# A decoder-layer kernel on one core: the first four adaLN weight chunks multiplied on TensorE in four column strips, and the weight stream started without a hold

## The reference

```
c_act = silu(c)                                   # c: (1, 1024)
mod   = c_act @ ada_w + ada_b                     # ada_w: 1024 x 6144
sh1, sc1, gt1, sh2, sc2, gt2 = split(mod, 6)      # 1024 each
h     = rmsnorm(x, norm_mix_g) * (1 + sc1) + sh1  # the modulated x
proj  = h @ w_in                                  # pool, q, k, v, z, rates and gates
...                                               # causal pooling and gated delta rule, residual
h     = rmsnorm(x, norm_ffn_g) * (1 + sc2) + sh2
x     = x + gt2 * moe(h)                          # top 4 of 32 experts, clamped SwiGLU
out   = rmsnorm(x, final_norm_g)
```

## Time and profile before

| what | value |
|---|---|
| median of three runs | 1480.12 us |
| profiled execution, its own time | 1478.27 us |
| its span, first to last instruction | 1476.7 us |
| TensorE busy, mean granted clock | 1327.4 us (90%), 0.971 |
| VectorE busy | 425.7 us (29%) |
| ScalarE busy | 175.0 us (12%) |
| moved by DMA | 484.38 MB, mean 328 GB/s |

### The profile page before, as it was taken

One profiled execution on the slowest core, in us unless ns is written; L12 is line 12 of the kernel. 1 busy time (PEld: TensorE's weight loads), 2 busy tenths in 40 slices (PEclk: granted clock), 3 DMA queues, 4 the chain that ended last, 5 costly groups with the idle time before them and its releaser, 6 DMA issues.

```text
span 1476.7 us, 17501 instructions
## 1 busy us (share of the span) xinstructions
PE 1327.4 (90%) x6612; PEld 673.9 (46%) x6612; DVE 425.7 (29%) x1020; ACT 175.0 (12%) x355; POOL 73.6 (5%) x67
## 2 busy tenths in 40 slices
PE   2799998989988899999899989998999899989996
PEld 1688866878876433333233323332333233323332
DVE  5588525363222421211121112111211121112112
ACT  1000111121201210110011001100110011001102
POOL 1010003333100000000000000000000000000000
PEclk8799989999999899999999999999999999999999
DMA  9968541010434199999999999999999999999994
GB/s 319 382 235 311 193 175 57 1 57 2 148 147 158 78 427 425 425 428 428 425 425 430 427 424 426 428 427 424 426 429 427 423 426 429 426 425 425 430 427 200
DMA packets 69510, 484.38 MB, mean 328 GB/s; under 512 B 4061, under 2 KB 4250, under 8 KB 35562
## 3 DMA queue, kind: packets, MB, share of 16 engines
q1 hardware_dynamic: 68448, 481.47, 79.3%
q0 software_dynamic: 560, 1.40, 0.4%
q10 hardware_dynamic: 474, 1.11, 0.2%
HBM read 482.92 MB, written 1.05 MB: 328 GB/s over the span
## 4 chain that ended last, share of the span: by engine, by line
DMA 50%; PE 43%; DVE 5%; ACT 1%; issue 1%; ACTq 0%; SPq 0%; DVEq 0%
DMA ring<-in_exp_w_dram 49%; PE bank L679 18%; PE bank L1041 12%; PE bank L1067 2%; PE bank L884 2%; PE bank L881 1%; PE bank L874 1%; DVE region_z L1181 1%; PE bank L1012 1%; PE bank L797 1%; PE bank L1079 1%; PE bank L701 1%; DMA work<-in_gdn_norm_g_dram 1%; DMA ring<-in_ada_w_dram 1%; PE bank L778 0%
## 5 line engine op out<-in xcount | busy, mean ns | idle before, releaser
L1041 PE MATMUL bank<-ring,work 128*64 128x512 f32 x2112 | 474.9, 598 | 63.7 <-DMA ring<-in_exp_w_dram 63.7
L1041 PEld LDWEIGHTS bank<-ring,work 128*64 128x64 f32 x2112 | 143.8, 137 | 391.1 <-issue 261.9
L1067 PE MATMUL bank<-ring,work 128*64 128x512 f32 x1056 | 233.9, 595 | 0.0
L679 PE MATMUL bank<-region_h,ring 128*128 128x256 f32 x832 | 187.4, 387 | 5.8 <-DVE region_h L1198 4.2
L679 PEld LDWEIGHTS bank<-region_h,ring 128*128 128x128 f32 x832 | 160.0, 194 | 29.4 <-DVE region_h L1198 4.3
L1067 PEld LDWEIGHTS bank<-ring,work 128*64 128x64 f32 x1056 | 72.9, 137 | 137.4 <-issue 137.4
L1510 DVE TENSOR_SCALAR work<-bank 128x256 f32<-128x256 f32 x66 | 27.6, 419 | 365.4 <-PE bank L1041 365.4
L638 ACT ACTIVATE work<-work 128x256 f32<-128x256 f32 x66 | 27.5, 416 | 782.6 <-DVE work L1510 782.6
L1537 DVE TENSOR_TENSOR work<-bank,work 128x512 f32<-128x512 f32 x33 | 22.8, 691 | 315.7 <-PE bank L1067 315.7
L1012 PE MATMUL bank<-qkv,work 128*64 128x512 f32 x272 | 65.7, 605 | 2.1 <-ACT qkv L614 2.1
L1079 PE MATMUL bank<-work 64*128 64x512 f32 x264 | 65.6, 615 | 0.8 <-DVE work L1537 0.8
(11 more groups left out here) (268 smaller groups left out, 958.1 us busy)
## 6 DMA issues: line engine op xcount, KB each, us to landing
ring<-in_exp_w_dram SPq DMA_DIRECT2D x198, 2048.0 KB, 24.0
ring<-in_w_in_dram SPq DMA_DIRECT2D x13, 2048.0 KB, 11.9
ring<-in_ada_w_dram SPq DMA_DIRECT2D x12, 2048.0 KB, 12.7
ring<-in_w_gdn_out_dram SPq DMA_DIRECT2D x2, 2048.0 KB, 7.8
ring<-in_w_out_dram SPq DMA_DIRECT2D x2, 2048.0 KB, 7.9
ring<-in_w_pool_out_dram SPq DMA_DIRECT2D x1, 2048.0 KB, 9.2
consts<-in_const_dram SPq DMA_DIRECT2D x1, 1153.0 KB, 6.4
region_x<-in_x_dram SPq DMA_DIRECT2D x2, 512.0 KB, 11.0
```

Source lines behind the costliest of these rows:

```text
L679: mm = nc.tensor.matmul(out_ap, w(k) if w else w_slot(n, j, k), rhs[:, k, :], start=(k == 0), stop=(k == kc - 1))
L1041: mm = nc.tensor.matmul(bank[b][h * SLOTS:(h + 1) * SLOTS, :], xT[:, c % 4, c // 4, :], slot_as(q, 2)[:, i, lo:lo + 512], start=False, sto ...
L1067: mm = nc.tensor.matmul(bank[2][o * SLOTS:(o + 1) * SLOTS, :], actT[:, b, c, h, :], slot_as(4 + b, 2)[:, h, lo:lo + 512], start=(b + h + c ...
```

## The change

- The wait of SyncE for the small rows is gone. `c` has a semaphore of its own (`c_in`), `ada_b` is issued by ScalarE, only the identity and the ones (128 KB) are loaded ahead of `x`, and the rest of the constants (2050 columns) follows the sixth chunk, under `tables_in`.
- The four `ada` chunks are cut otherwise: chunk q holds rows 256q to 256q+255 of the first 2048 columns, in pieces of 8 KB.
- `ada_rows` multiplies each on TensorE: the stationary operand is a column of `c_act` repeated 32 times, the moving one 512 weight columns, and the four groups of 512 columns go to the four 32-column strips of the array, all into bank 5. VectorE's sums over these chunks are gone; ScalarE copies bank 5 to `ada_row` (in unused columns of `qkv`), and four matmuls with four columns of the identity turn it into the 16 columns of `mod`.
- `c` is transposed by itself, the transposes of `x` go to banks 1, 2, 3 and 7, and the small rows are turned between the third and the fourth chunk.
- `vec_hT` is raised after each of the eight feature tiles, and the first eight matmuls of the first projection wait for one tile each.

The diff, cut to its core:

```diff
@@ sync @@
-            sp.dma_start(rows[ROW_C:ROW_C + 8, :], c.rearrange("b (r n) -> (b r) n", n=P)).then_inc(rows_in, 16)
-            sp.dma_start(rows[ROW_ADA_B:ROW_ADA_B + 48, :],
-                         ada_b.rearrange("l (r n) -> (l r) n", n=P)).then_inc(rows_in, 16)
-            sp.dma_start(consts[:, :], const).then_inc(const_in, 16)
+            sp.dma_start(rows[ROW_C:ROW_C + 8, :], c.rearrange("b (r n) -> (b r) n", n=P)).then_inc(c_in, 16)
+            sp.dma_start(consts[:, 0:2 * P], const[:, 0:2 * P]).then_inc(const_in, 16)
             for t in range(T):
                 sp.dma_start(xt[:, t, :], x[0, t * P:(t + 1) * P, :]).then_inc(x_in, 16)
-            sp.wait_ge(rows_in, 16 * 10)
...
+                if n == RING - 1:
+                    sp.dma_start(consts[:, 2 * P:CONST_W], const[:, 2 * P:CONST_W]).then_inc(tables_in, 16)
@@ chunks @@
-        chunks = [("ada", cut(ada_w, CW * i)) for i in range(4)]
+        chunks = [("ada", ada_w[0, 2 * P * q:2 * P * (q + 1), 0:2 * D].rearrange("(c p) n -> p c n", p=P))
+                  for q in range(4)]
@@ scalar @@
-            act.wait_ge(vec_cols, 1)
-            nc.scalar.activation(c_act[:, :], cols[:, ROW_C:ROW_C + 8], ACT.Silu).then_inc(act_c, 1)
+            act.wait_ge(pe_c, 1)
+            nc.scalar.activation(c_act[:, :], bank[7][:, 0:8], ACT.Silu).then_inc(act_c, 1)
...
+            act.wait_ge(used[3], 1)
+            nc.scalar.activation(ada_row, bank[5][:, :], ACT.Copy).then_inc(act_adarow, 1)
@@ tensor @@
+            def ada_rows(q):
+
+                arrived(q)
+                w = slot_as(q % RING, 2)
+                for i in range(2):
+                    for j in range(4):
+                        mm = nc.tensor.matmul(bank[5][32 * j:32 * j + 32, :],
+                                              c_act[:, 2 * q + i:2 * q + i + 1].to_broadcast([P, 32]),
+                                              w[:, i, CW * j:CW * (j + 1)],
+                                              start=(q + i == 0), stop=(q == 3 and i == 1))
+                mm.then_inc(used[q % RING], 1)
+
...
+            ada_rows(0)
+            pe.wait_ge(vec_xn, 2)
+            for f in range(KC):
+                for t in range(T):
+                    mm = nc.tensor.transpose(turned(f)[:, t * P:(t + 1) * P], xt[:, t, f * P:(f + 1) * P], ident)
+            mm.then_inc(pe_xT, 1)
+            ada_rows(1)
+            ada_rows(2)
+            pe.wait_ge(rows_in, 16 * 9)
...
+            ada_rows(3)
+            pe.wait_ge(act_adarow, 1)
+            for i in range(4):
+                mm = nc.tensor.matmul(bank[4][:, 4 * i:4 * i + 4], ada_row[:, i * P:(i + 1) * P],
+                                      ident.rearrange("p (j a) -> p a j", j=4)[:, 0, :], start=True, stop=True)
+            mm.then_inc(pe_adacol, 1)
...
-            for n in range(4):
-                ada_columns(n, bank[5][:, 4 * n:4 * n + 4])
-
-            pe.wait_ge(vec_hT, 1)
@@ vector @@
-            dve.wait_ge(act_c, 1)
-            for n in range(4):
-                ada_sums(n, chunk_no["ada"][n])
-
-            dve.wait_ge(pe_ada, 4)
-            link(tt(mod[:, 0:16], bank[5][:, 0:16], cols[:, 0:16], ALU.add))
+            dve.wait_ge(pe_adacol, 1)
+            link(tt(mod[:, 0:16].rearrange("p (j i) -> p i j", j=4),
+                    bank[4][:, 0:16].rearrange("p (i j) -> p i j", i=4),
+                    cols[:, ROW_ADA_B:ROW_ADA_B + 16].rearrange("p (j i) -> p i j", j=4), ALU.add))
...
             for f in range(KC):
-                ins = ts(hT[:, f, :], pair(f // 2)[:, f % 2, :], scale1[:, f:f + 1], mod[:, f:f + 1], ALU.mult, ALU.add)
-            ins.then_inc(vec_hT, 1)
+                ins = ts(hT[:, f, :], turned(f), scale1[:, f:f + 1], mod[:, f:f + 1], ALU.mult, ALU.add)
+                ins.then_inc(vec_hT, 1)
```

More of the change, by code:

```diff
@@ L53 @@
 COL_GATE = COL_BA + 2 * HEADS
-ROW_ADA_B = 0
-ROW_C = 48
+ROW_C = 0
+ROW_ADA_B = 8
 ROW_G1 = 56
@@ L244, in pair, with turned @@
             return bank[i][:, :].rearrange("p (a s) -> p a s", a=2)
+        def turned(f):
+            return pair((1, 2, 3, 7)[f // 2])[:, f % 2, :]
         def quad(i):
@@ L251, in program @@
         rows_in = sem("rows_in")
+        c_in = sem("c_in")
+        tables_in = sem("tables_in")
         x_in = sem("x_in")
@@ L260, in program @@
         vec_chain = sem("vec_chain")
+        pe_c = sem("pe_c")
+        act_adarow = sem("act_adarow")
+        pe_adacol = sem("pe_adacol")
         pe_rows = sem("pe_rows")
         vec_cols = sem("vec_cols")
+        vec_eps = sem("vec_eps")
         act_c = sem("act_c")
@@ L398, in program @@
         chunks += [("w_out", cut(w_out, CW * i)) for i in range(2)]
+        parts_of = {"ada": 2, "pool_out": 4}
         chunk_no = {}
@@ L445, in _ @@
                     sp.wait_ge(used[n % RING], n // RING)
-                dst = slot_as(n % RING, 4) if kind == "pool_out" else ring[:, n % RING, :, :]
+                dst = ring[:, n % RING, :, :]
+                if kind in parts_of:
+                    dst = slot_as(n % RING, parts_of[kind])
                 sp.dma_start(dst, src).then_inc(landed[n % RING], 16)
+                if n == RING - 1:
+                    sp.dma_start(consts[:, 2 * P:CONST_W], const[:, 2 * P:CONST_W]).then_inc(tables_in, 16)
             def stream(n):
@@ L515, in _ @@
         def _(act):
+            act.dma_start(rows[ROW_ADA_B:ROW_ADA_B + 48, :],
+                          ada_b.rearrange("l (r n) -> (l r) n", n=P)).then_inc(rows_in, 16)
             for j in range(TAPS):
@@ L674, in carry, with project @@
                     mm.then_inc(used[done_chunk.pop() % RING], 1)
-            def project(out_ap, n, j, rhs, kc=KC, w=None):
+            def project(out_ap, n, j, rhs, kc=KC, w=None, each=None):
                 for k in range(kc):
+                    if each:
+                        pe.wait_ge(each, k + 1)
                     mm = nc.tensor.matmul(out_ap, w(k) if w else w_slot(n, j, k), rhs[:, k, :],
@@ L722, in pair_of @@
                     pe.wait_ge(*released[i - 4])
+                elif i:
+                    pe.wait_ge(vec_hT, KC)
                 for a in range(2):
-                    mm = project(pair(i % 4)[:, a, :], n, j + a, rhs, kc, w and (lambda k, a=a: w(k, a)))
+                    mm = project(pair(i % 4)[:, a, :], n, j + a, rhs, kc, w and (lambda k, a=a: w(k, a)),
+                                 vec_hT if i + a == 0 else None)
                 mm.then_inc(pe_pair, 1)
@@ L1157, in _ @@
             copy, recip = nc.vector.tensor_copy, nc.vector.reciprocal
-            link(nc.vector.memset(small[:, 16:17], EPS))
-            dve.wait_ge(const_in, 16)
-            ts(small[:, 17:18], const_tile("qscale"), EPS, None, ALU.mult)
+            nc.vector.memset(small[:, 16:17], EPS).then_inc(vec_eps, 1)
+            dve.wait_ge(act_xrms, 1)
+            link(recip(stat[:, 0, 2:4], stat[:, 0, 2:4]))
+            for t in range(T):
+                ts(xt[:, t, :], xt[:, t, :], stat[:, 0, 2 + t:3 + t], None, ALU.mult).then_inc(vec_xn, 1)
             dve.wait_ge(pe_rows, 1)
@@ L1165, in _ @@
             dve.wait_ge(vec_cols, 2)
-            dve.wait_ge(act_xrms, 1)
-            link(recip(stat[:, 0, 2:4], stat[:, 0, 2:4]))
-            for t in range(T):
-                ts(xt[:, t, :], xt[:, t, :], stat[:, 0, 2 + t:3 + t], None, ALU.mult).then_inc(vec_xn, 1)
             def ada_sums(n, place):
@@ L1243, in _ @@
             counts = const_tile("count").rearrange("p (g n) -> p g n", g=4)
-            dve.wait_ge(const_in, 16)
+            dve.wait_ge(tables_in, 16)
+            ts(small[:, 17:18], const_tile("qscale"), EPS, None, ALU.mult)
             for i, w in enumerate(WINDOWS):
```

25 lines of the change are left out of this document (13 added, 12 removed).

## The result

The changed kernel takes 1469.14 us (median of six runs, 1466.08 to 1471.08) against 1478.51 (six runs, 1477.54 to 1480.53). The ratio is 0.9932, with a 95% interval of 0.9917 to 0.9947, so it is faster by 0.5 to 0.8%. The profiled execution took 1469.21 us with a span of 1467.6, 9.1 less than before. The forecast of 1465.0 had the direction and the range right, and promised 13.3 us where 9.4 came.

What follows compares the result with a forecast made beforehand. Small rows' wait, then VectorE, bound the kernel ahead of 48.2 us, TensorE behind. Starting projections at 36.2 gains 12.0, the clock 1.3: 13.3 off 1478.3 gives 1465.0 us, range 1459 to 1471.

Steps and rivals of the forecast that it cites:

- The frame: Whole kernel: small rows' wait, then VectorE, bound it ahead of 48.2 us, TensorE behind; a microsecond gained there reaches the end.
- the ring: Weight chunks' slots: must keep up for the gain to reach the end; seventh chunk had 2.0 us of cover.
- The first chunk's landing: First ada chunk in the front: lands at 14.5 us, with 3.5 us counted for the other two queues.
- 1468.8: Time in us if an ada chunk took 5.9 us at the skill's 358 GB/s, the four 3.8 more.
- The path behind the fourth chunk: Last ada chunk's matmuls to first tile, at 1.2 GHz: 6.9 us, from 29.3 to a start at 36.2.
- the first rival: TensorE's clock stays high or is back before the projections: path 4.3 us, start 34.7, time 1462.2; chance 0.24.
- the first of the signs of being wrong: At the projections' start: the first projection waits for the fifth chunk, so the clock or the path was better.
- the stretch without a dip from 3 us on: Sign of being right, in the front: DMA at about 388 GB/s or more from 3 us on.
- The clock: First two projection chunks: low clock costs 2.6 us; rising earlier after the start wins half, 1.3.
- the hold was not what held: Front: other queues' tiny pieces, not SyncE's wait, set the first chunk's landing at 19.9; start 41.5, 1470.3 us; chance 0.09.
- The slower rival: Front: poor strip overlap and a low clock make TensorE the bound, 7.1 us a chunk, start 53.4, 1483.5; chance 0.05.
- The release by tile: Modulated x before the first projection: makes the last step 0.5 us rather than 3.7, worth 3.2.

Runs made afterwards that it cites:

- The late loads: Changed kernel with GpSimd's six early loads (pool, rates' and router weights, three broadcasts) issued after the ada rows are turned: 1464.70 us.
- the spread of those matmuls: Rates' narrow matmuls spread between projection pairs: on the late loads alone 1462.13 us; on late loads, fillers and loads moved further back 1460.16 us.
- the hold put back: Changed kernel with SyncE again issuing the first chunk only when c and nine small rows have landed: 1467.74 us.
- overlap taken away: Changed kernel with all four column groups of each ada chunk on the first column strip: 1483.35 us, ratio to before 1.0033.

## Why the prediction was right, and where its sizes were off

*The frame* held in part. What is gained ahead of the experts is gained at the end (9.1 and 9.1), VectorE's sums were the bound behind the first chunk, the ring kept up, and the strips overlap. Beside GpSimd's loads the hold did not bind: the kernel before without it is no faster, and the changed kernel with it no slower. What set the first chunk's landing was what the DMA engines had to carry beside it.

*The first chunk's landing* was the mis-sized term: 14.5 in the sum, 18.70 measured. The prediction counted the other queues by their share of engine time, 3.5 us, and added it. The late loads show what GpSimd's loads cost where they stand: 6.6 us for the first chunk, nearly double, since less moves while they are under way, and later chunks move before the first is complete. These 3.1 us are most of the error; the other 1.1 is there with the late loads too (12.09, where 14.5 less 3.5 would be 11.0). The error of 4.2 was carried to the fourth chunk (33.5 for 29.3) and the fifth (38.9 for 34.7); the steps between were right, 5.0 for the 4.9 of an ada chunk and 5.4 for 5.4. So the 8 KB pieces run at some 424 GB/s here, and the 358 GB/s for a core's share of the Trainium skill (DMA: Bandwidth & Descriptors, Specifications), by which I weighed 1468.8, is not what these windows show. That 1468.8 came so close to the measured 1469.14 is luck.

*The path behind the fourth chunk* was 6.9 in the sum and is 38.24 - 33.54 = 4.7: the clock was high there, as the first rival had it, and the multiplication took 1.92. The start was forecast at 36.2 behind the path and came at 38.95 behind the fifth chunk, whose landing was not the bound in the forecast. That is the first of the signs of being wrong that the prediction named, and the stretch without a dip from 3 us on did not come either (193 GB/s at 10 to 12). Part of the late landing was hidden by luck: with the forecast path the start would have been 33.5 + 6.9 = 40.4.

*The clock.* Forecast half of 2.6 won, measured 1.2 (29.34 for 30.55). In front 9.25 + 1.2 = 10.5 came for 13.3. *The rest of the gap*, 1.7 us, is the deeper fall of the clock at the rates' matmuls, of which some 0.3 comes back later; the spread of those matmuls shows that they cause the fall. Its depth changes from run to run, and the profile of the changed kernel had a deep one.

*The rival "the hold was not what held"* had 0.09 and 1470.3, and stands nearest to the truth: the time came within 1.2 us of it, and the hold put back costs nothing. It was set too low since I took the share of engine time for the whole price. *The slower rival* needed poor overlap; with overlap taken away the kernel is slower than before by 0.33%, so it decides as it said. It also had x's transposes at 7.0 us, twice the 3.49 of the earlier trace rows, which were themselves at the low clock for the most part. *The release by tile* was put at 3.2 and is worth 2.2 at the start: with it the start waits for the fifth chunk (38.95) and not for the first tile (38.24).

## What to carry to other kernels

Small-piece loads beside a stream cost more than their share of engine time (6.6 us for 3.5 here), and the first transfer, for which everything waits, pays it: put them where the stream rests, before asking whether it can start earlier, and look at what they then stand ahead of. A release or a hold is to be tried with and without its neighbours; here the release of the hold was worth nothing beside the small loads and 2.5 us without them, and the late loads gained in the time only once the hold was gone. Once a front is bound by loading, fill TensorE's waits or spread its narrow matmuls, as a fall of its clock (1.7 us) costs as much as the waits of 1.2 to 1.9 us.

## What the runs showed of the hardware that was not expected

- The granted clock reads 1.00 from the start of a profile, and the records do not run so. In the changed kernel the first chunk's 16 records take 3.25 us with 1.00 beside them, the same at 33.54 take 1.92; in the kernel before without its hold the column steps take 1.86 where the reading is 1.00, and 0.95 later. The 3.49 us of x's transposes in the earlier trace rows were mostly at the low clock too (1.97 at 21.89 after). So the "2.4 GHz until 26.7" of the prediction was a reading, not a speed.
- Issued 6.9 us earlier, the same chunk was there 1.6 us later (18.70 against 17.10), and in the kernel before, issued 9.1 us earlier, it landed 2.0 us later (21.9 against 19.9).
- 32 records of 16 columns in a row, with TensorE busy all the time, let its clock fall: the granted clock is 0.50 from 131 to 137 us in the changed kernel, and the next 64 records take 15.5 to 16.8 us in the profiles, instead of 14.06. Eight of them at a time between wide ones don't.
- Four column strips of 32 give 3.6 times one strip (1.92 for 6.96).
